# First block of a two-layer trunk kernel: order of its loads, its sum of squares and its projections

## The chip, the cores and the metric

The kernel runs on the 8 cores of one Trainium2 chip. Each core takes one prompt of 2048 tokens and 32 sample tokens, and no core needs another's data. The metric is device time in microseconds of the slowest core, median over runs. A profile is one execution on the slowest core.

## The reference

Two layers, each a mixer and an MLP with residual adds, for 2080 tokens of 1024 channels per core:

```
h = rmsnorm(x, norm1_g)
u, q, k, v, gb, gc, gh = split(h @ w_in)          # 256, 3 x 384, 3 x 384 columns
y_pool = pool_mix(u)                              # window sums over 2, 4, 8, 16 tokens, then 64 x 64 products
y_attn = dilated attention of q, k, v             # three groups of two heads, QK-norm, partial rotary
z = gc * gh;  y_conv = gb * conv_mix(z)           # causal width-3 convolution
x = x + concat(y_pool, y_attn, y_conv) @ w_out
x = x + square(relu(rmsnorm(x, norm2_g) @ w_up)) @ w_down
```

rmsnorm(x, g) is x * rsqrt(mean(x*x) + 1e-6) * g. Each layer also returns the last rows of its pooling, convolution and key/value histories.

## The kernel before, in words

Tokens lie along the free axis, channels on the 128 partitions. The 2080 tokens are cut into 5 blocks of 416 (BL), and a block of x is 8 chunks of 128 channels, one 128x416 tile each. For every block of layer 0 the mixer does this: the chunks of x are loaded; each is scaled by the norm's gain and cast to bf16 into HT (cast1, line 859 on VectorE and GpSimd, 860 on ScalarE); each is squared, and a matmul with a matrix of ones sums the squares over partitions and chunks into one PSUM bank (sumsq, lines 1002 and 1003 for block 0, 1011 and 1012 for the others); ScalarE takes Ln (1054) and Exp (1066) of that sum, which gives 1/rms; and a Square (1103, in rv) gives its square. The projections run on the unnormalised bf16 tile HT: proj (1172) is 8 accumulating matmuls per 128 output columns. Their results are multiplied by 1/rms, or its square, when they leave PSUM. The convolution item (conv_item) first multiplies the "c" projection by the square of 1/rms (1288), then by the "h" projection (1300, 1302), runs the convolution (860, 1313, 1315), multiplies by 1/rms (1318) and by the "b" projection (1322). pool_item does the same for the pooling columns with "p" projections (1228, 1233, 1238, 1251). The token sums (1072) give the same 1/rms per token for the attention's q, k and v, whose projections are line 1357.

All loads of x but two, and all weights, are issued by GpSimd (POOL) on its DMA queue; the weights are cast to bf16 on the way. Block 0 of x is loaded in four quarters of two chunks (load_x, line 939): the first two quarters by SyncE (SP), the last two by GpSimd. Blocks 1 to 4 come in two halves of four chunks. The "c", "h", "p" and "b" weights come as 11 pieces w_a of 128 columns (load_piece, line 964), called c0, h0, c1 and so on. Small loads go by SP: smallc (gains and constants, 922), sconv and spool (histories, 1185 and 1187), qk_g (953). The squares of block 0 are written to Z0, the place of x that later holds V tiles; a memset of those (1803) on GpSimd has to wait until they are read.

The program is emitted by a planner. Items are generators that yield operations with a priority; the planner keeps one queue per engine, models durations and DMA time, and appends whatever is ready and most urgent to that engine's fixed order. An operation given as "any" of several engines goes to the first that is free. Hardware then runs each engine's list in order, with semaphore waits where data or space is shared. So a changed rule or cost moves instructions on all engines far behind the place of the change. Waits of the planner on its own events (ev) order the lists; they make no semaphore wait by themselves.

## Time and profile before

| | |
|---|---|
| median of 3 runs | 1437.58 us (1434.56 to 1439.44) |
| the profiled execution's own time | 1430.84 us |
| its span, slowest core | 1429.3 us (cores 1418.1 to 1429.3) |
| TensorE busy | 1380.4 us, 97% of the span |
| VectorE, ScalarE, GpSimd busy | 821.7, 705.7, 385.1 us |
| share of the chain that ended last on TensorE | 89% |
| mean granted TensorE clock, by core | 0.992 to 0.997 |

The span runs from the first to the last instruction of a core; what is outside it is 1.5 us here. The page has seven parts: busy times, the span in 40 slices, DMA queues, the chain of work that ended last, the costliest groups of instructions and the DMA issues; the trace answers questions on any stretch, tile or line. A load's time to landing counts from the start of its issue. An f32 matmul leaves two records in the trace. A granted clock of 1.00 is 2.4 GHz, 0.50 is 1.2 GHz.

### The profile page before, as it was taken

What the parts mean: (1) busy time and instruction counts of PE and PEld (TensorE: products, weight loads), DVE (VectorE), ACT (ScalarE), POOL (GpSimd) and SP (SyncE); (2) the same over time, 40 slices, a digit from 0 to 9 for tenths busy, and PEclk for the clock granted to TensorE, in tenths of its full rate; (3) what the DMA queues carried; (4) which work ended last, traced back from release to release, by engine and by line L of the source; (5) the groups of instructions that cost most, each with busy time, mean ns of one, the idle gap of its engine ahead of it and who ended that gap; (6) DMA issues with size and microseconds to landing.
All of it is one profiled execution on the core that took longest, in us unless ns stands there. A gap on an engine that the chain in (4) does not pass through costs nothing.

```text
span 1429.3 us, 28093 instructions; the slowest of 8 cores (1418.1 to 1429.3 us)
## 1 busy us (share of the span) xinstructions
PE 1380.4 (97%) x8921; PEld 787.5 (55%) x8921; DVE 821.7 (57%) x1534; ACT 705.7 (49%) x1495; POOL 385.1 (27%) x561
## 2 busy tenths in 40 slices
PE   6999998899999999999999999899999999999998
PEld 2555665455555555555555566555555555555554
DVE  1878876774444444446677788867644444444443
ACT  3657665664244342436646566557444343433522
POOL 4566747340000000002236666653000000000000
PEclk8999999999999999999999999999999999999999
DMA  9851447960652490143245052399037228200122
GB/s 202 204 83 33 89 107 166 230 89 1 120 77 77 92 180 1 19 85 95 73 98 126 26 88 55 95 261 164 3 82 114 77 64 133 76 1 1 49 97 96
DMA packets 81679, 133.33 MB, mean 93 GB/s; under 512 B 14008, under 2 KB 70520, under 8 KB 81152
## 3 DMA queue, kind: packets, MB, share of 16 engines
q0 software_dynamic: 53952, 79.29, 30.4%
q1 hardware_dynamic: 18880, 49.10, 11.6%
q10 hardware_dynamic: 8704, 3.15, 0.9%
q8 instruction: 75, 1.23, 0.4%
q14 instruction: 68, 0.56, 0.1%
HBM read 159.63 MB, written 47.90 MB: 145 GB/s over the span
## 4 chain that ended last, share of the span: by engine, by line
PE 89%; DMA 4%; issue 2%; POOL 2%; DVE 1%; ACT 1%; SPq 0%; DVEq 0%; POOLq 0%; ACTq 0%
PE psum L1767 32%; PE psum L1743 31%; PE psum L1357 9%; PE psum L1172 9%; PE psum L1720 4%; DMA big<-xin 1%; PE psum L1589 1%; DMA big<-xin_r 1%; POOL big L859 1%; DMA big<-xpark 1%; PE psum L1480 1%; DMA kv_p<-big 1%; PE psum L1003 1%; PE psum L1564 0%; PE psum L1614 0%
## 5 line engine op out<-in xcount | busy, mean ns | idle before, releaser
L1743 PE MATMUL psum<-big 128*128 128x416 bf16 x2560 | 457.6, 339 | 2.3 <-DVE big L1755 1.5
L1767 PE MATMUL psum<-big 128*128 128x416 bf16 x2560 | 456.6, 339 | 0.0
L1743 PEld LDWEIGHTS psum<-big 128*128 128x128 bf16 x2560 | 249.2, 98 | 202.7 <-issue 6.2
L1767 PEld LDWEIGHTS psum<-big 128*128 128x128 bf16 x2560 | 249.8, 98 | 199.8 <-issue 1.7
L1758 ACT ACTIVATE big<-big 128x416 f32<-128x416 f32 x291 | 159.6, 549 | 403.8 <-DVE big L1755 402.9
L1755 DVE TENSOR_TENSOR big<-psum,big 128x416 f32<-128x416 f32 x320 | 188.8, 591 | 231.5 <-PE psum L1743 173.5
L1770 DVE TENSOR_TENSOR big<-psum,big 128x416 f32<-128x416 f32 x320 | 189.0, 591 | 226.7 <-PE psum L1767 226.1
L1759 ACT ACTIVATE big<-big 128x416 bf16<-128x416 f32 x320 | 175.0, 549 | 49.0 <-POOL big L1757 6.1
L1172 PE MATMUL psum<-big 128*128 128x416 bf16 x880 | 172.3, 345 | 5.5 <-ACT big L1093 1.4
L1357 PE MATMUL psum<-big 128*128 128x384 bf16 (+1 forms) x816 | 140.5, 326 | 2.3 <-ACT big L1576 2.3
L860 ACT ACTIVATE big<-big 128x416 bf16<-128x416 f32 (+5 forms) x139 | 87.3, 636 | 82.6 <-DVE big L1724 36.1
L1172 PEld LDWEIGHTS psum<-big 128*128 128x128 bf16 x880 | 83.7, 100 | 72.1 <-issue 14.0
L975 POOL DMA_DIRECT2D big<-w_up x32 | 24.6, 777 | 312.7 <-PE psum L1743 301.7
L1357 PEld LDWEIGHTS psum<-big 128*128 128x128 bf16 (+1 forms) x816 | 77.7, 98 | 53.6 <-issue 4.1
L1720 PE MATMUL psum<-big 128*128 128x416 bf16 x480 | 86.9, 339 | 7.5 <-DVE big L1724 7.5
L859 POOL TENSOR_SCALAR big<-big 128x416 bf16<-128x416 f32 (+5 forms) x43 | 60.7, 1413 | 86.3 <-DVE big L1724 30.8
L1720 PEld LDWEIGHTS psum<-big 128*128 128x128 bf16 x480 | 46.2, 98 | 45.6 <-issue 10.6
L1724 DVE TENSOR_TENSOR big<-psum,big 128x416 f32<-128x416 f32 x80 | 46.1, 587 | 30.1 <-PE psum L1720 22.5
L1419 POOL TENSOR_TENSOR big<-big 128x128 f32<-128x128 f32 (+1 forms) x87 | 48.0, 552 | 28.6 <-DVE big L1418 15.5
L1424 ACT ACTIVATE big<-psum 128x512 f32<-128x512 f32 (+1 forms) x54 | 30.7, 569 | 48.3 <-PE psum L1357 44.5
L975 POOL DMA_DIRECT2D big<-w_down x32 | 24.4, 773 | 72.9 <-PE psum L1767 72.9
L1313 DVE SCALAR_TENSOR_TENSOR big<-big 128x416 f32<-128x416 f32 (+1 forms) x60 | 41.2, 693 | 1.4 <-POOL big L859 0.4
(144 smaller groups left out, 1155.2 us busy)
## 6 DMA issues: line engine op xcount, KB each, us to landing
big<-w_up POOLq DMA_DIRECT2D x32, 512.0 KB, 13.5
big<-w_down POOLq DMA_DIRECT2D x32, 512.0 KB, 10.5
kv_s<-c SPq DMA_DIRECT2D x8, 2040.0 KB, 12.4
big<-xin_r POOLq DMA_DIRECT2D x10, 832.0 KB, 8.7
xpark<-big SPq DMA_DIRECT2D x10, 832.0 KB, 4.1
big<-xpark POOLq DMA_DIRECT2D x10, 832.0 KB, 13.9
yout<-big SPq DMA_DIRECT2D x20, 416.0 KB, 2.4
big<-xin POOLq DMA_DIRECT2D x8, 832.0 KB, 13.0
```

The costliest lines, as they stand in the source:

```text
L859: f = lambda e: e.tensor_scalar(out=out, in0=in_, scalar1=g, scalar2=None, op0=ALU.mult)
L860: return anyof(act(n, lambda e: e.activation(out=out, in_=in_, func=AF.Copy, scale=g), r, w, True), dvec(n, f, r, w), pool(n, f, r, w, False))
L975: yield ops(ldc(lambda e: e.dma_start(out=dst, in_=src), 1048576, 2048, w=[(nm, i, h)], slot=(nm, i, h)))
L1172: bi = yield late(1, lambda bi: pe([(BL, lambda e, d=d: e.matmul(bank(bi)[:, 0:BL], lhsT=wa(l, nm, i, d), rhs=HT[:, d, BL * b:BL * b + BL] ...
L1357: pb0 = yield late(J, lambda pb0: pe([(384, lambda e, d=d, j=j, jj=jj: e.matmul(bank(pb0 + jj)[0:R, 0:384].rearrange("p (k n) -> p k n", k ...
L1720: bi = yield late(1, lambda bi: pe([(BL, lambda e, c=c: e.matmul(bank(bi)[:, 0:BL], lhsT=WO[c // 2][:, c % 2, 128 * oc:128 * oc + 128], rh ...
L1743: bi = yield late(1, lambda bi: pe([(BL, lambda e, d=d: e.matmul(bank(bi)[:, 0:BL], lhsT=WU[i][:, d, 128 * fc:128 * fc + 128], rhs=HT[:, d ...
L1755: yield ops(dve(BL, lambda e: e.tensor_tensor(out=rl, in0=bank(bi)[:, 0:BL], in1=VB[v], op=ALU.mult), [("ps", bi), kvb(v)], [kr]))
L1758: yield ops(anyof(act(BL, lambda e: e.activation(out=rl, in_=rl, func=AF.Relu), [kr], [kr]), dvec(BL, f, [kr], [kr]), pool(BL, f, [kr], [k ...
L1759: yield ops(act(BL, lambda e: e.activation(out=AT[a][:, fc, :], in_=rl, func=AF.Square), [kr], [("at", a, fc)]))
L1767: bi = yield late(1, lambda bi: pe([(BL, lambda e, f=f: e.matmul(bank(bi)[:, 0:BL], lhsT=WD[i][:, f, 128 * oc:128 * oc + 128], rhs=AT[a][: ...
L1770: yield ops(dve(BL, lambda e: e.tensor_tensor(out=X[:, s, oc, :], in0=bank(bi)[:, 0:BL], in1=X[:, s, oc, :], op=ALU.add), [("ps", bi), ("x ...
```

## The change

It has five parts. (1) SP's second quarter of x is issued right behind the first: sconv, spool and qk_g are held by the planner until all of block 0's loads are done in its model. (2) The squares of block 0 are added in pairs on VectorE, and four f32 matmuls with ones take the place of eight. (3) Block 0's casts may go to ScalarE and VectorE, no longer to GpSimd. (4) Weight pieces h0 and c1 are issued ahead of block 1 of x. (5) The "h" projection of block 0's convolution items is its own item, which needs neither the norm nor the history. The planner's model of early DMA time is also changed (a factor of 1.35 and a floor at 3.3 us).

```diff
--- before.py
+++ after.py
@@ -457,9 +457,12 @@
         self.busy[eng] += cost
         if len(op) > 4 and eng != "dve":
             t, n, d = op[4]
-            if max(self.dma_free, self.now) < 4.5:
-                t *= 2.0
-            if eng == "pool":
+
+            cold = self.now < 4.5 and t > 1.0
+            if cold:
+                t *= 1.35
+                self.dma_free = max(self.dma_free, 3.3)
+            if eng == "pool" or cold:
                 self.dma_free = max(self.dma_free, self.now) + t
                 self.bulk = d
                 done = self.dma_free + 2.0
@@ -996,13 +999,16 @@
         if l == 0 and which == 0 and b == 0:
 
             bi = yield acq(BANKS)
-            for c in range(8):
-                yield wait(src[c])
-                t, k = Z0[:, 0, c, :], ("x", SV, c)
-                yield ops(act(BL, lambda e: e.activation(out=t, in_=X[:, si, c, :], func=AF.Square), [("x", s, c)], [k]))
-                K.spawn(later(pe([(BL * 4, lambda e, c=c, t=t: e.matmul(bank(bi)[:, 0:BL], lhsT=ONESR[:, :].bitcast(F32), rhs=t, start=(c == 0), stop=(c == 7)),
-                                   ["onesr", k], [("ps", bi)])]), ev("nadd", l, which, b, c)), 1)
-            yield wait(*[ev("nadd", l, which, b, c) for c in range(8)])
+            def pair(c):
+                t, k, t0, k0 = Z0[:, 0, c, :], ("x", SV, c), Z0[:, 0, c - 1, :], ("x", SV, c - 1)
+                yield wait(src[c - 1], src[c])
+                yield ops(*[act(BL, lambda e, t_=t_, c_=c_: e.activation(out=t_, in_=X[:, si, c_, :], func=AF.Square), [("x", s, c_)], [k_]) for t_, k_, c_ in ((t0, k0, c - 1), (t, k, c))])
+                yield ops(dve2(BL, lambda e: e.tensor_tensor(out=t, in0=t, in1=t0, op=ALU.add), [k, k0], [k]))
+                yield ops(pe([(BL * 4, lambda e: e.matmul(bank(bi)[:, 0:BL], lhsT=ONESR[:, :].bitcast(F32), rhs=t, start=(c == 1), stop=(c == 7)), ["onesr", k], [("ps", bi)])]))
+                K.fire(ev("nadd", l, which, b, c))
+            for c in (1, 3, 5, 7):
+                K.spawn(pair(c), 2 if c < 7 else 1)
+            yield wait(*[ev("nadd", l, which, b, c) for c in (1, 3, 5, 7)])
         elif l == 0 and which == 0:
             bi = yield acq(BANKS)
             for c in range(8):
@@ -1034,7 +1040,8 @@
 
         yield wait(src, *before)
         o, i = HT[:, c, BL * b:BL * b + BL], X[:, si, c, :]
-        yield ops(scaled(BL, o, i, NG[:, l, 0, c:c + 1], [("x", s, c), "ng"], [("ht", b, c)]))
+        op = scaled(BL, o, i, NG[:, l, 0, c:c + 1], [("x", s, c), "ng"], [("ht", b, c)])
+        yield ops(anyof(*op[1][:2]) if l == b == 0 else op)
         K.fire(ev("hc", l, b, c))
 
     def cast_watch(l, b):
@@ -1180,7 +1187,7 @@
         return ap.rearrange("p (r n) -> p r n", n=4)
 
     def load_hist(l, s):
-        yield wait(ev("free", l, s))
+        yield wait(*([ev("free", l, s)] if l else [ev("xr", 0, 0, c) for c in range(8)]))
         if s == SC:
             yield ops(ld(lambda e: e.dma_start(out=ZS[:, 0:2], in_=sconv[l]), 12288, 96, w=[("zs", cc) for cc in range(3)], slot="zs"))
         else:
@@ -1279,6 +1286,13 @@
         Zv = Z[cc]
         kz, ks = ("z", cc), ("zs", cc)
         cw = lambda k: CONVW[:, l, cc, k:k + 1]
+        hb = []
+
+        def ahead():
+            hb.append((yield from proj(l, "h", cc, b)))
+        if l == b == 0:
+
+            he = K.spawn(ahead(), 1000)
         bc = yield from proj(l, "c", cc, b)
         yield wait(ev("rv", l, b))
         ci = yield acq(PCA)
@@ -1296,7 +1310,11 @@
         K.fire(ev("cg", l, b, cc))
         if b == 0:
             yield wait(ev("hist", l, SC))
-        bh = yield from proj(l, "h", cc, b)
+        if l == b == 0:
+            yield wait(he)
+        else:
+            hb.append((yield from proj(l, "h", cc, b)))
+        bh = hb[0]
         o2 = [dve(L, lambda e: e.tensor_tensor(out=Zv[:, 2:2 + L], in0=bank(bh)[:, o:BL], in1=gs[:, o:BL], op=ALU.mult), [("ps", bh), kg], [kz])]
         if b == 0:
             o2.append(dve(32, lambda e: e.tensor_tensor(out=ZS[:, 2:10, cc, :], in0=n4(bank(bh)[:, 0:32]), in1=n4(gs[:, 0:32]), op=ALU.mult), [("ps", bh), kg], [ks]))
@@ -1806,7 +1824,7 @@
     def mixer(l):
         base = 1000 * l
         K.spawn(zero_q(l), base + 1)
-        K.spawn(seq([] if l == 0 else [ev("qk", l - 1, blk, g, pr) for blk in range(4) for g in range(3) for pr in range(2)] + [ev("qk", l - 1, None, g, 0) for g in range(3)], load_gqk(l)), base + 1)
+        K.spawn(seq([ev("xr", 0, 0, c) for c in range(8)] if l == 0 else [ev("qk", l - 1, blk, g, pr) for blk in range(4) for g in range(3) for pr in range(2)] + [ev("qk", l - 1, None, g, 0) for g in range(3)], load_gqk(l)), base + 1)
         K.spawn(v_ones(l), base + 1)
         for s in (SC, SP_):
             K.spawn(load_hist(l, s), base + 0.01)
@@ -1910,7 +1928,7 @@
     K.spawn(consts(), 0)
     x_loads = lambda b: [load_x(b, h) for h in range(2 if b else 4)]
     w = lambda *a: [load_piece(0, x[0], int(x[1])) for x in a]
-    K.spawn(loads([], 0, *x_loads(0), *w("c0"), *x_loads(1), *w("h0", "c1", "h1", "c2", "h2"), *w("p0", "p1", "b0"), load_pw(0), *w("b1", "b2"),
+    K.spawn(loads([], 0, *x_loads(0), *w("c0", "h0", "c1"), *x_loads(1), *w("h1", "c2", "h2"), *w("p0", "p1", "b0"), load_pw(0), *w("b1", "b2"),
                   *x_loads(2), *x_loads(3), load_atc(), *[load_wq(0, i) for i in range(3)], *x_loads(4)), 0)
     K.spawn(loads([ev("ht", 0, 4), ev("sq", 0, 4)], 3, *[load_wo(0, i) for i in range(3)]), 3)
     for l in range(DEPTH):
```

The first place is the start of TensorE's list. Lines 1003 and 1007 are the matmul with ones of block 0's squares (before, and in the changed file), 1172 and 1179 a projection, 1072 and 1079 the token sums, 1012 and 1018 the matmul with ones of block 1. Before:

```order
L1003 MATMUL psum<-big,onesr 128x416 x6
L1172 MATMUL psum<-big 128x416 x8
L1003 MATMUL psum<-big,onesr 128x416 x2
L1072 MATMUL psum<-onesr,big 128x1 x3
L1072 MATMUL psum<-onesr,big 32x1
L1012 MATMUL psum<-sqr,onesr 128x416 x2
L1172 MATMUL psum<-big 128x416 x8
L1012 MATMUL psum<-sqr,onesr 128x416
L1172 MATMUL psum<-big 128x416 x8
```

Now:

```order
L1007 MATMUL psum<-big,onesr 128x416 x2
L1179 MATMUL psum<-big 128x416 x8
L1007 MATMUL psum<-big,onesr 128x416 x2
L1179 MATMUL psum<-big 128x416 x16
L1079 MATMUL psum<-onesr,big 128x1 x3
L1079 MATMUL psum<-onesr,big 32x1
L1018 MATMUL psum<-sqr,onesr 128x416 x3
L1179 MATMUL psum<-big 128x416 x16
```

One projection stood between six and two matmuls with ones; now one stands between two and two, and two more projections (16 matmuls) stand ahead of the token sums, which need the norm's Ln. At the same place VectorE's list; 859 and 862 are casts, 1006 the new add of two squares, 1288 and 1302 the first multiply of a "c" projection. Before:

```order
L859 TENSOR_SCALAR big<-big 128x416 x8
L1288 TENSOR_TENSOR big<-psum,big 128x416 x2
L1300 TENSOR_TENSOR big<-psum,big 128x384
L1302 TENSOR_TENSOR big<-psum,big 128x8x4
L1300 TENSOR_TENSOR big<-psum,big 128x384
```

Now:

```order
L862 TENSOR_SCALAR big<-big 128x416 x2
L1006 TENSOR_TENSOR big<-big 128x416
L862 TENSOR_SCALAR big<-big 128x416
L1006 TENSOR_TENSOR big<-big 128x416
L862 TENSOR_SCALAR big<-big 128x416 x2
L1006 TENSOR_TENSOR big<-big 128x416 x2
L1302 TENSOR_TENSOR big<-psum,big 128x416 x2
```

The eight casts were one run; now the first add stands behind the second cast, which needs the second quarter of x, and the adds alternate with the casts. The second place is the start of GpSimd's list: 939 and 942 are loads of x, 964 and 967 weight pieces, 859 and 862 casts, 1803 and 1821 the memset over the squares. Before:

```order
L939 DMA big<-xin 128x832 x2
L964 DMA big<-w_a 128x1024
L859 TENSOR_SCALAR big<-big 128x416
L939 DMA big<-xin 128x1664 x2
L859 TENSOR_SCALAR big<-big 128x416
L964 DMA big<-w_a 128x1024 x3
L859 TENSOR_SCALAR big<-big 128x416
L964 DMA big<-w_a 128x1024
```

Now:

```order
L942 DMA big<-xin 128x832 x2
L967 DMA big<-w_a 128x1024 x3
L942 DMA big<-xin 128x1664 x2
L967 DMA big<-w_a 128x1024
L1821 MEMSET big 128x8x64
L967 DMA big<-w_a 128x1024
L1819 MEMSET big 128x2x64 x2
L967 DMA big<-w_a 128x1024
L1819 MEMSET big 128x2x64
L862 TENSOR_SCALAR big<-big 128x416
```

Five loads that stood between casts are now issued ahead of any cast; the first cast on GpSimd is one of block 1, with the memset ahead of it. The third place is GpSimd's list at the loads of blocks 2 and 3 of x, 1245 being the first add of the pooling item (1238 before), which waits for VectorE's line 1240 (1233 before). Before:

```order
L939 DMA big<-xin 128x1664
L1290 MEMSET big 128x2
L939 DMA big<-xin 128x1664
L1227 MEMSET big 128x15
L939 DMA big<-xin 128x1664
L1227 MEMSET big 128x15
L939 DMA big<-xin 128x1664
L859 TENSOR_SCALAR big<-big 128x416
L925 DMA big<-atc 128x864
```

Now:

```order
L942 DMA big<-xin 128x1664 x2
L1234 MEMSET big 128x15
L942 DMA big<-xin 128x1664
L1234 MEMSET big 128x15
L1245 TENSOR_TENSOR big<-big 128x398
L942 DMA big<-xin 128x1664
L862 TENSOR_SCALAR big<-big 128x416
L928 DMA big<-atc 128x864
L948 DMA big<-w_q 128x3072
```

The last half of block 3 was issued straight behind a memset; it now stands behind the pooling add, and the loads of the constants (925, 928) and the first w_q (948) behind it.

## Rows read from the trace of the kernel before

**Rows 1.** The page, part 1: engine, busy us (share of the span), instructions
```profile
PE 1380.4 (97%) x8921; PEld 787.5 (55%) x8921; DVE 821.7 (57%) x1534; ACT 705.7 (49%) x1495; POOL 385.1 (27%) x561
```

**Rows 2.** Windows view: stretch, its length, busy of five engines, PEclk, DMA share, GB/s
```profile
14.00:17.00 3.00, 1.94 (x3) 1.17 (x4) 1.26 (x4) 3.00 (x7) 0.27 (x1) 0.53 0.99 323
17.00:20.70 3.70, 3.70 (x6) 1.50 (x5) 1.68 (x4) 1.18 (x3) 3.70 (x6) 0.50 1.03 190
...
24.00:27.90 3.90, 1.74 (x10) 1.27 (x11) 0.00 (x0) 3.71 (x11) 1.98 (x7) 0.99 1.06 164
27.90:30.40 2.50, 2.49 (x9) 1.13 (x9) 0.59 (x1) 1.19 (x3) 0.00 (x0) 0.50 1.11 159
...
82.40:300.00 217.60, 204.59 (x1728) 123.75 (x1727) 168.79 (x334) 140.09 (x340) 128.97 (x199) 0.99 0.57 119
```

**Rows 3.** Timeline of the first 7 us, loads of x (start, duration, engine)
```profile
1.66 1.30 POOL L939 DMA_DIRECT2D big<-xin  x2 [0.25 <-issue]
...
2.93 0.43 SPq L939 DMA_DIRECT2D big<-xin  x1
```

**Rows 4.** DMA view, loads issued at 1.6 to 8.6 us: KB, us to landing
```profile
big<-xin POOLq DMA_DIRECT2D x1, 416.0 KB, 6.8
big<-xin POOLq DMA_DIRECT2D x1, 416.0 KB, 8.4
big<-xin SPq DMA_DIRECT2D x1, 416.0 KB, 10.8
big<-w_a POOLq DMA_DIRECT2D x1, 256.0 KB, 11.0
...
big<-xin POOLq DMA_DIRECT2D x1, 832.0 KB, 8.0
```

**Rows 5.** Timeline of 13 to 29 us; brackets: idle time before, and its releaser
```profile
13.84 0.64 ACT L860 ACTIVATE big<-big 128x416 bf16<-128x416 f32 x1 [5.97 <-DMA big<-xin]
15.06 5.89 PE L1003 MATMUL psum<-big,onesr 128*128 128x416 f32 x8 [4.38 <-ACT big L1002]
22.27 1.56 PE L1003 MATMUL psum<-big,onesr 128*128 128x416 f32 x4
23.98 0.61 ACT L1054 ACTIVATE big<-psum,big 128x416 f32<-128x416 f32 x1 [5.80 <-PE psum L1003]
24.73 0.95 PE L1072 MATMUL psum<-onesr,big 128*128 128x1 f32 x8 [0.91 <-ACT big L1054]
26.34 0.16 ACT L1092 ACTIVATE big<-psum 128x3 f32<-128x3 f32 x1
27.68 0.53 ACT L1011 ACTIVATE sqr<-big 128x416 fp32r<-128x416 f32 x1
27.91 2.93 PE L1172 MATMUL psum<-big 128*128 128x416 bf16 x8 [1.44 <-ACT big L1093]
28.75 0.59 DVE L1288 TENSOR_TENSOR big<-psum,big 128x416 f32<-128x416 f32 x1 [8.65 <-ACT big L1103]
```

**Rows 6.** The chain that ended last, 31 to 83 us: start, us, what
```profile
31.19 1.50 PE psum L1172 x8
...
59.45 10.13 DMA big<-xin
...
82.59 2.62 PE psum L1357 x16
```

**Rows 7.** Timeline of VectorE at 38 and 42 us
```profile
38.03 0.58 DVE L1318 TENSOR_TENSOR big<-big 128x416 f32<-128x416 f32 x1
...
42.61 0.54 DVE L1233 TENSOR_TENSOR big<-psum,big 128x384 f32<-128x384 f32 x1
```

**Rows 8.** DMA view, loads issued at 23.2, 24.8 and 25.4, 56.4 us
```profile
big<-w_a POOLq DMA_DIRECT2D x1, 256.0 KB, 12.7
big<-xin POOLq DMA_DIRECT2D x2, 832.0 KB, 19.6
big<-w_q POOLq DMA_DIRECT2D x1, 768.0 KB, 8.8
```

## Prediction

> **What bounds the kernel now.** First the page's busy times: TensorE is busy 1380.4 us of a span of 1429.3 [rows 1], so 48.9 us of idle time, and the matmuls that ran at the lower clock, are all that a new order can win. Next the windows, which say where these lie: from 82.4 to 300 us TensorE idles 217.60 - 204.59 = 13.0 us; from 14 to 30 us it is half idle or at 0.50 to 0.53 of its clock (1.2 GHz) most of the time [rows 2]. A change that touches only the first block of layer 0 directly must earn its time there and keep it through the rest of that layer's mixer.
>
> Then the timeline of the start. A load's landing is its issue plus its time. GpSimd's two quarters of x, issued together from 1.66 to 2.96 (the second near 2.3), took 6.8 and 8.4 us and were there at 8.5 and 10.7; SP's second quarter, issued at 2.93 behind two small loads, took 10.8 and landed at 13.7 [rows 3, 4]. ScalarE's cast at 13.84 had idled 5.97 us for it, and TensorE idled 4.38 us for the squares behind it. TensorE then did eight records (four f32 matmuls) in 5.89 us, the first projection, and from 22.27 the last four records; the norm's Ln started at 23.98 and VectorE's first multiply only at 28.75, for ScalarE had put other work between Ln and the Square on which it waits [rows 5]. The chain gives the state at 32.7 us (31.19 + 1.50) [rows 6]: TensorE has then done block 0's sums of squares and token sums, three projections and three squares of block 1. I call this the mark; the changed list of TensorE, read above, holds the same set up to its third matmul of block 1.
>
> **The change step by step.** All times are estimates from these rows.
>
> *SP's second quarter.* It is issued at about 1.95, and shares the DMA engines with GpSimd's quarters alone. Nearest row: GpSimd's second quarter, as large and second in its queue as well, landed at 10.7; I take that. Bounds: 8.5 (GpSimd's first quarter) and 13.7 (no change) [rows 4]. The trace shows what the small loads do to a queue only by this one load. sconv, spool and qk_g now share with c0: it landed at 2.94 + 11.0 = 13.9 beside the same loads, and I leave it there.
>
> *Pairs instead of eight matmuls.* Four adds on VectorE at 0.58 us (line 1318, same form [rows 7]), which was 1.26 us busy in the 3 us from 14 [rows 2]: no cost, but the first add stands behind the cast that waits for the second quarter. So: cast 10.7 to 11.1, add to 11.7, second add at 12.7, the last at about 15.4. Two matmuls with ones are four records of 0.74 us at the lower clock (5.89/8), from 11.8 to 14.7. The first projection needs c0 (13.9) and casts that are done by 13.6, and costs 2.93 us at the lower clock (line 1172 at 27.91 [rows 5]), to 17.6. Before, the records ahead of that projection ran at 0.50 of the clock [rows 2] and the four behind it took 0.39 us each, the higher clock's price [rows 5]; with the same order of work I take the same prices, so 1.56 us for the last two matmuls, to 19.2. Ln starts 0.15 us later, as it did before (22.27 + 1.56 to 23.98), at 19.3.
>
> The casts taken from GpSimd go to ScalarE and VectorE, which wait for x there. No cost.
>
> *Ln to the first multiply.* ScalarE's list now has Ln, Exp and Square in a row: 0.61 + 2 x 0.53 and 0.3 of waits, so VectorE's multiply starts near 21.3 instead of 28.75, 7.4 us earlier.
>
> *Projections ahead of the norm.* h0 and c1 stand behind c0 on the DMA queue. Four quarters and c0 (4 x 416 KB and 512 KB, cast to 256 on the way) had landed at 13.9, some 200 KB per us from 3 us on; so 2.6 us each: 16.5 and 19.1. TensorE needs them at 19.2 and 20.7. Sixteen matmuls, 2 x 1.50 [rows 6]: to 22.2; token sums, 0.95 [rows 5]: to 23.1. Here a wait is new: the third square of block 1 stands on ScalarE behind the reads of the token sums, and from the first of these (26.34) to that square's end (27.68 + 0.53) took 1.9 us before [rows 5]; one more square of 0.53 and waits follow, so its matmul ends at 26.2. Block 1's first half, landing at 8.55 + 8.0 = 16.6 before, has two pieces ahead of it now: 21.8 at most, in time. The mark is reached at 26.2, **6.5 us earlier**. With the bounds of the second quarter this is 7.3 (c0 then holds the projection) or 3.5; if the clock stayed at 0.50 throughout, 5.86 instead of 3.0 for two projections and 2.95 instead of 1.56 make it 2.2.
>
> On clock and gaps the Trainium skill, "TensorE: Matmul & The Clock Gate", section "HAM oscillation — how this bites in real kernels", says that waits between groups of matmuls throttle the array again. By that rule the new wait near 24 us speaks for the low end, 2.2; the rows agree in kind (0.50 at 27.9, after 1.74 us busy out of 3.9 [rows 2]), but the one fall in these rows came after longer idle time, so I stay with the higher clock and count the low end with the first rival below.
>
> *GpSimd's queue.* Issuing h0, c1 and block 1 at once, earlier than before, costs nothing: the DMA engines are 0.99 to 1.11 busy from 14 to 30 us [rows 2] either way. The last pieces land as before, b2 at 23.2 + 12.7 = 35.9 [rows 8]; shifted by 6.5 us TensorE wants it near 39. The last half of block 3 now stands behind the pooling add, thus behind VectorE's line 1233, at 42.61 before [rows 7]. With 7.4 us off and some 3 us of block 1's casts put in between, that is 38.3, issue at 39.5. It was issued at 25.4 and landed near 45.0 (the two halves' median was 19.6 us [rows 8]) for want of DMA bandwidth, not for its issue. After 39.5 and another 8.0, the time of block 1's first half, it lands at 47.5: 2.5 us later, in a chain with room: the third w_q landed at 56.4 + 8.8 = 65.2 and the last block of x at 59.45 + 10.13 = 69.6, both held by late issues from GpSimd, while the attention's first projection came at 82.59 [rows 6, 8]. At zero, then.
>
> *The rest.* Behind the mark all lists are shuffled as far as layer 0's MLP. I see nothing that TensorE does more or less of; I take 0.5 us off for new waits. **Sum: 6.5 - 0.5 = 6.0 us**, against the profiled execution's 1430.84: 1424.8. That execution lies 6.7 us below the median of the runs shown; against the median, 1437.58 - 6.0 = **1431.6 us**. A measurement of this kernel tells a change from none at about 0.3%, 4.3 us.
>
> **Rivals.**
>
> *Given back.* DMA work is the same and was never idle early; if x and w_q, not TensorE's start, time what comes up to 82.6, the 6.5 us turn into waits before it. For it: DMA busy above 0.99 [rows 2], the late loads [rows 6, 8]. Against it: 13 us lie between the last block's landing and the attention's start. Also here: half of the gain lost to a shuffled attention stage. Also here: a clock that stays low, 2.2 us less waits. Left: about 1.5 us, 1436. The Trainium skill, "DMA: Bandwidth & Descriptors", section "Issuing engines are not separate DMA queues", says that loads of all issuing engines interleave on the same 16 DMA engines, so that another queue or an earlier issue saves only the issue; by that rule the second quarter gains only what the small loads lose. Only SP's one load (10.8 beside 8.4) bears on it here.
>
> *The small loads are not held.* The lists make no semaphore wait for them, so they run behind the second quarter at once, beside c0. Were c0 3 us later for it, the projection and the mark would be too: 6.5 - 3 = 3.5, 1434.1, the low end of the forecast's own range, where I count it with a chance of 0.08.
>
> *More.* The attention stage idles 13.0 us; a start 7 us earlier for VectorE, with 168.79 of 217.6 us busy there [rows 2], may take a third of it as well: 6.0 + 4 = 10, 1427.6.
>
> *Slower: the pooling add holds the loads.* GpSimd's queue runs dry if the add comes after 36 us (block 3's first half lands near 24.8 + 19.6 = 44.4, less 8.0). If VectorE reaches line 1233 at 45.6, that is 42.61 and the 3 us of casts with no gain before, block 3's half is issued near 47 and lands at 55; three w_q of 4.8 us (1.5 MB at the 323 GB/s of [rows 2]) end at 70 instead of 65.2, and block 4's first half lands at 73 instead of 69.6. With casts and squares behind it TensorE loses some 5 us: 1442.6. Against it: VectorE's start hangs on the second quarter and c0 alone. It decides when the add comes later than about 43.
>
> **How the numbers follow.** Forecast (gain of 3.5 to 9 us, 1428.6 to 1434.1): 0.50 with the small loads' case, of which 0.44 is beyond 4.3 us. Given back: 0.30, all within 0.3%. More: 0.10. Slower: 0.10, all beyond it. Faster 0.44 + 0.10 = 0.54, same 0.06 + 0.30 = 0.36, slower 0.10. The range, 1424.5 to 1441.5, takes in the forecast, nearly all of "given back", most of "more" and the milder "slower" cases.
>
> **What would show it.** Right: SP's second quarter lands by 11; four new adds and eight f32 records; Ln near 19.3; VectorE's first multiply near 21.3; the mark near 26; the attention's first projection near 76; and from 82 on no more idle time than 13 us. Wrong: Ln after 22 with the second quarter still late, or the first projection of attention within 2 us of 82.6 (given back), or a dry DMA queue between 44 and 50 us (slower).

## The result, and the profile after

The changed kernel takes **1426.61 us** (median of three runs, 1426.24 to 1426.70) beside 1438.38 for the kernel before (four runs, 1434.56 to 1439.44): a ratio of 0.9922, 95% interval 0.9899 to 0.9946, so about 11.2 us less by the ratio (8 to 14.5). Executions in which a die was disturbed are left out of all medians here, and for e2 and e9 below, whose profiled execution was one of them, the profile's figures are means over the four cores of the other die. On the three chips of the experiments (e1 to e4, e5 to e8, e9 to e12) the kernel before had medians of 1433.5 to 1433.9, and the changed one, measured again beside e6 to e8, 1425.61: 8.2 us less, ratio 0.9942 (0.9927 to 0.9956). Forecast were 6.0 us less. The profiled execution took 1426.61 us, its span is 1425.1.

Busy times hardly moved, by 3.3 us at most, as against [rows 1]. Page of the changed kernel, part 1:

```profile
PE 1378.4 (97%) x8913; PEld 787.2 (55%) x8913; DVE 825.0 (58%) x1531; ACT 708.4 (50%) x1501; POOL 381.8 (27%) x562
```

Windows of the changed kernel, columns as in [rows 2]; the last stretch begins at its first attention projection and is as long as that of before:

```profile
14.00:17.00 3.00, 3.00 (x8) 1.06 (x7) 1.19 (x2) 0.86 (x2) 2.03 (x6) 1.00 1.05 221
17.00:20.70 3.70, 3.70 (x16) 2.02 (x15) 0.00 (x0) 1.09 (x2) 0.65 (x1) 1.00 1.00 334
24.00:27.90 3.90, 2.88 (x8) 1.51 (x9) 2.54 (x8) 3.35 (x10) 3.90 (x10) 0.58 1.08 172
...
72.20:289.80 217.60, 202.32 (x1706) 122.64 (x1705) 166.15 (x324) 140.65 (x345) 123.59 (x198) 0.99 0.60 118
```

From 14 to 20.7 us TensorE now works without a gap, where it had idle time or worked at half clock. The 1.00 of the first of these rows is not borne out by its matmuls: the first projection takes 2.92 us for eight (below), the price that the kernel before paid at 0.50 (2.93 at 27.91 [rows 5]), and sixteen behind it take 2.98. At 24 us there is a new hole, and the clock falls behind it (0.58). In the long stretch it idles 15.3 us, where it was 13.0.

Timeline of the start, the changed kernel's core 0; it answers to [rows 3, 5]. Line 1061 is Ln, 1302 the first multiply, 1018 the second block's matmul with ones:

```profile
1.51 0.90 SPq L942 DMA_DIRECT2D big<-xin  x2
...
11.05 0.64 ACT L863 ACTIVATE big<-big 128x416 bf16<-128x416 f32 x1 [1.91 <-DMA big<-xin]
...
12.14 3.11 PE L1007 MATMUL psum<-big,onesr 128*128 128x416 f32 x4 [12.14 <-DVE big L1006]
...
15.05 2.92 PE L1179 MATMUL psum<-big 128*128 128x416 bf16 x8
...
17.80 1.56 PE L1007 MATMUL psum<-big,onesr 128*128 128x416 f32 x4
...
19.20 2.98 PE L1179 MATMUL psum<-big 128*128 128x416 bf16 x16
...
19.51 0.61 ACT L1061 ACTIVATE big<-psum,big 128x416 f32<-128x416 f32 x1 [4.66 <-PE psum L1007]
...
21.51 0.59 DVE L1302 TENSOR_TENSOR big<-psum,big 128x416 f32<-128x416 f32 x1 [5.95 <-ACT big L1110]
...
25.02 1.12 PE L1018 MATMUL psum<-sqr,onesr 128*128 128x416 f32 x2 [1.74 <-ACT sqr L1017]
...
25.94 4.01 PE L1179 MATMUL psum<-big 128*128 128x416 bf16 x16
```

The second quarter is cast at 11.05 instead of 13.84, Ln comes at 19.51 instead of 23.98, the multiply at 21.51 instead of 28.75, and the third matmul of the second block's squares (the mark) ends at 25.02 + 1.12 = 26.14 instead of 32.7.

GpSimd's list around the last half of block 3, changed kernel:

```profile
37.23 1.05 POOL L1245 TENSOR_TENSOR big<-big 128x398 f32<-128x398 f32 x1 [9.27 <-DVE big L1240]
38.23 0.58 POOL L942 DMA_DIRECT2D big<-xin  x1
...
46.31 1.58 POOL L862 TENSOR_SCALAR big<-big 128x416 bf16<-128x416 f32 x1 [1.62 <-DMA big<-xin]
...
56.92 0.60 POOL L942 DMA_DIRECT2D big<-xin  x1
...
57.97 0.58 POOL L942 DMA_DIRECT2D big<-xin  x1
```

The pooling add holds the load, as foreseen, until 38.23; what it brings is there at 46.3. The last block of x is issued at 56.92 and 57.97, where [rows 6] has 59.45.

The third view to read is that of the cores, for the metric is the slowest of eight. Kernel before, then the changed one:

```profile
core 0: 1419.7 us, clock 0.997
core 1: 1427.9 us, clock 0.992
core 2: 1427.2 us, clock 0.993
core 3: 1418.2 us, clock 0.996
...
core 6: 1429.3 us, clock 0.993
core 7: 1418.1 us, clock 0.993
```

```profile
core 0: 1425.1 us, clock 0.995
core 1: 1418.1 us, clock 0.997
core 2: 1423.8 us, clock 0.995
core 3: 1416.8 us, clock 0.995
...
core 6: 1420.0 us, clock 0.996
core 7: 1424.6 us, clock 0.996
```

Of each pair (0 and 1, 2 and 3, and so on) one core ends late, now the one, now the other. Over 26 executions of the kernel before (those beside the first four experiments) the quicker core of a pair has a mean of 1420.4 us, the slower of 1430.0, and the slowest of the eight 1432.2. Over the five of the changed kernel beside the fifth these are 1417.4, 1422.8 and 1424.0: the quicker ones gained 3.0 us, the slower ones 7.2, the slowest of the eight 8.2.

### The profile page after: what moved, and what is told of

Its sections match the earlier page's. It is cut to its first block, busy times and chain, and to the rows that moved or that the text cites. A ratio compares the mean times of both kernels' runs of the same rounds, so it can differ in the third digit from the quotient of the medians.

```text
span 1425.1 us, 28092 instructions; the slowest of 8 cores (1415.6 to 1425.1 us)
## 1 busy us (share of the span) xinstructions
PE 1378.4 (97%) x8913; PEld 787.2 (55%) x8913; DVE 825.0 (58%) x1531; ACT 708.4 (50%) x1501; POOL 381.8 (27%) x562
## 4 chain that ended last, share of the span: by engine, by line
PE 87%; DMA 5%; POOL 2%; issue 2%; DVE 2%; ACT 2%; DVEq 0%; ACTq 0%; SPq 0%; POOLq 0%
PE psum L1785 32%; PE psum L1761 31%; PE psum L1179 8%; PE psum L1375 8%; PE psum L1738 4%; DMA big<-xin 2%; PE psum L1607 1%; DMA big<-xin_r 1%; POOL big L862 1%; DMA big<-xpark 1%; DMA big<-vspill 1%; PE psum L1498 1%; ACT big L1442 0%; PE psum L1582 0%; PE psum L1079 0%
## 5 line engine op out<-in xcount | busy, mean ns | idle before, releaser
L1375 PEld LDWEIGHTS psum<-big 128*128 128x128 bf16 (+1 forms) x816 | 77.9, 98 | 55.5 <-issue 7.0
L862 POOL TENSOR_SCALAR big<-big 128x416 bf16<-128x416 f32 (+5 forms) x41 | 56.8, 1388 | 75.1 <-DVE big L1742 38.0
L1742 DVE TENSOR_TENSOR big<-psum,big 128x416 f32<-128x416 f32 x80 | 46.4, 588 | 28.5 <-PE psum L1738 18.4
L1437 POOL TENSOR_TENSOR big<-big 128x128 f32<-128x128 f32 (+1 forms) x83 | 45.4, 546 | 20.1 <-DVE big L1436 10.3
## 6 DMA issues: line engine op xcount, KB each, us to landing
big<-xpark POOLq DMA_DIRECT2D x10, 832.0 KB, 14.5
```

The lines of the kernel that those rows point to most:

```text
L862: f = lambda e: e.tensor_scalar(out=out, in0=in_, scalar1=g, scalar2=None, op0=ALU.mult)
L1375: pb0 = yield late(J, lambda pb0: pe([(384, lambda e, d=d, j=j, jj=jj: e.matmul(bank(pb0 + jj)[0:R, 0:384].rearrange("p (k n) -> p k n", k ...
```

## The experiments

Three theories stood at the start. A: the gain is the earlier front (the work of the first block up to the mark), the same on all cores. B: what decides is the landing of the last block of x, on the slower core of each pair. C: it is the new order of the attention stage.

Most edits move instructions in the finished lists and leave all others where they are; waits follow the data. The table gives means over the cores of the profiled execution: the mark here is the time when five projections of the first block and five matmuls of the second block's squares are done (it suits all orders), then the first and the last attention projection; the last column is the median time.

| kernel | mark | first | last | median us |
|---|---|---|---|---|
| before (profiled as above) | 35.3 | 80.3 | 227.5 | 1433.5 to 1433.9 |
| changed (profiled as above) | 29.6 | 70.8 | 223.2 | 1426.6 |
| e1 before, last block of x earlier | 35.8 | 78.5 | 224.8 | 1430.6 |
| e2 before, SP's new order (cores 0 to 3) | 31.7 | 78.7 | 226.0 | 1431.8 |
| e3 changed, SP's old order | 31.5 | 70.9 | 223.2 | 1426.5 |
| e4 changed, held | 33.3 | 73.1 | 225.7 | 1429.2 |
| e5 changed, again | 28.5 | 69.6 | 222.1 | 1425.6 |
| e6 changed, nothing ahead of the norm | 33.1 | 73.9 | 226.2 | 1428.9 |
| e7 changed, no pairs | 30.1 | 70.3 | 223.3 | 1427.3 |
| e8 changed, last block of x earlier | 28.4 | 68.4 | 219.8 | 1424.4 |
| e9 changed, four parts undone (cores 4 to 7) | 38.1 | 79.2 | 231.9 | 1436.9 |
| e10 changed, lists dealt anew | 29.2 | 69.7 | 215.3 | 1432.8 |
| e11 e8 and squares first | 27.8 | 68.8 | 220.1 | 1426.1 |
| e12 e8 and x read again earlier | 28.8 | 68.0 | 219.5 | 1422.4 |

**e1**, GpSimd's list of the kernel before:

```diff
+L939 DMA big<-xin 128x1664 x2
 L945 DMA big<-w_q 128x3072
...
-L939 DMA big<-xin 128x1664 x2
```

> The kernel before, with one thing moved: the two loads of the fifth block of x stand on GpSimd's queue ahead of the third load of w_q and of the pooling work behind it, nothing else. Theory A (the front): the gain comes from the first block's norm being over earlier; nothing before 55 us is touched here, so the time stays that of the kernel before, 1438 us within 1.5. Theory B (the landing): on the cores that end last, the attention's first projection (82 to 83.4 us on four cores, 78 on the other four) hangs on the landing of the fifth block (69.6 on core 6, 65.8 on core 0); issued some 3 us earlier it lands by 66.5 on every core, all cores come to the first projection by 79.5, and the slowest core's time falls by 3 to 5 us, to 1433 to 1435. A third view (the third part of w_q is now the late one): the same or slower, with the tensor engine waiting for that load at 85 to 95 us.

The cores did come together at the first attention projection: 76.8 to 79.5 us instead of 77.9 to 83.4. Casts of the last block, core 0 and core 6 of e1:

```profile
64.33 1.83 POOL L859 TENSOR_SCALAR big<-big 128x416 bf16<-128x416 f32 x1 [4.17 <-DMA big<-xin]
```

```profile
64.30 1.33 POOL L859 TENSOR_SCALAR big<-big 128x416 bf16<-128x416 f32 x1 [3.66 <-DMA big<-xin]
```

Before, core 0 had its first half at 65.98 and core 6 at 69.75. So theory B is right up to 80 us. At the end the median is 3.3 us less (1430.6 beside 1433.9), the lower end of what B said: eight of the nine executions lie at 1429.3 to 1431.5. The ninth took 1447.3; with it the ratio, 0.9991 (0.9966 to 1.0015), can't be told from nothing. The two profiled executions do not show the gain: they took 1430.87 and 1430.84 us, the latter near the lowest of the 26 (1430.4), and the last output projection starts at 276.5 to 284.5 in e1, at 277.2 to 285.2 before. Where the lead gets to behind the attention stays open.

**e2 and e3**, SP's list, the same exchange in the one kernel and undone in the other:

```diff
 L939 DMA big<-xin 128x832
+L939 DMA big<-xin 128x832
 L1185 DMA big<-sconv 128x24
 L1187 DMA big<-spool 128x120
-L939 DMA big<-xin 128x832
```

> The kernel before, with one thing moved: on SP's queue the second quarter of x stands directly behind the first, ahead of the loads of sconv and spool. Theory A: the second quarter lands near 11 instead of 13.7, the squares and the eight matmuls with ones that wait for it run up to 2.7 us earlier, Ln starts at 21.3 to 22.5 instead of 23.98, and the third matmul of the second block's squares near 30 instead of 32.7; all that follows keeps this, 1438 becomes 1435 to 1436. Theory B: GpSimd's queue and the landing of the fifth block move by under 1 us, and the time by under 1 us. If the two old queue neighbours cost nothing, the second quarter lands at 13.7 as before and nothing moves.

> The changed kernel, with SP's queue as before the change: the loads of sconv and spool stand between the first and the second quarter of x, nothing else. Theory A: the second quarter lands near 13.7 instead of 11.0, the last pair's work on it is 2.7 us later, Ln moves from 19.5 to 21.5 or later, the third matmul of the second block's squares from 26.1 to 28 or 29, and the time from 1426.6 to 1428.5 to 1429.5. Theory B: the time stays within 1 us of 1426.6, since the fifth block of x still lands near 65.5. A third view (the first block's order of quarters is such that the second one isn't the last): Ln stays at 19.5 and nothing moves.

e2: Ln at 20.9 on core 1, where that core had 23.6; the mark 3.6 us earlier, the time 2 us less (ratio 0.9988, 0.9976 to 1.0001, which just reaches no change), at the low end of theory A's 2 to 3. But the landing of the last block's first half moved as well, from 67.1 to 65.2 in the mean of these four cores, where B expected under 1 us: the front moves that landing, and A and B are not independent. e3 misses theory A's number: the second quarter came late, Ln at 21.82 on core 5 (19.32 in the changed kernel), the mark 3 us later than in e5, but the first attention projection and the time stay within 1.3 us. Three microseconds at the mark are worth 0.8 there, as theory B has it. Timeline of e3, core 5:

```profile
14.16 0.64 ACT L863 ACTIVATE big<-big 128x416 bf16<-128x416 f32 x1 [5.36 <-DMA big<-xin]
...
21.82 0.61 ACT L1061 ACTIVATE big<-psum,big 128x416 f32<-128x416 f32 x1 [3.85 <-PE psum L1007]
```

**e4**, ScalarE's list:

```diff
+L1005 ACTIVATE big<-big 128x416 x11
 L1005 ACTIVATE big<-big 128x416 x2
```

> The changed kernel, with ScalarE held for some 6 us ahead of the first block's first square (it computes that square eleven times more, each behind the one before), all lists otherwise the same. Theory A: Ln goes from 19.5 to near 25.5, the third matmul of the second block's squares from 26.1 to near 32.5, the attention's first projection from 72 to 78, and the time from 1426.6 to 1432.5 to 1433: each microsecond of the front is one of the end. Theory B: the hold costs at the end what it does to the landing of the fifth block of x; if GpSimd still issues it before 58 us and it lands by 66.5, the time rises by under 2 us. Theory C (the order of the attention stage is what gained): the time rises by under 3 us whatever the front does, since idle time in the attention stage takes the rest up.

The hold was partly covered, since the second quarter lands at 10.7 anyway: Ln moved by 2.6 us on core 1 (19.11 to 21.73) and 3.9 on core 5. Against e5 the mark is 4.9 us later, the first attention projection 3.5, the time 3.6. About three quarters pass.

**e5**, no edit.

> The changed kernel itself, with the same lists on every engine, beside the kernel before on one chip: what the difference is here, core by core. Theory B (the slower core of each pair): the quicker core of each pair (0 and 1, 2 and 3, ...) gains 2 to 3 us against the kernel before, the slower one 5 to 6, and the slowest of the eight 7 to 8: near 1426.6 where the kernel before has 1434. Theory A alone (the front, the same for all cores): all cores gain the same 6.5 us.

As theory B has it (numbers above): not all cores gain alike. That fits B; it does not by itself show that the last block of x is the cause.

**e6**, TensorE's list:

```diff
-L1179 MATMUL psum<-big 128x416 x16
 L1079 MATMUL psum<-onesr,big 128x1 x3
 L1079 MATMUL psum<-onesr,big 32x1
-L1018 MATMUL psum<-sqr,onesr 128x416 x3
-L1179 MATMUL psum<-big 128x416 x16
+L1018 MATMUL psum<-sqr,onesr 128x416 x2
+L1179 MATMUL psum<-big 128x416 x8
+L1018 MATMUL psum<-sqr,onesr 128x416
+L1179 MATMUL psum<-big 128x416 x24
```

> The changed kernel, with two projections (h0 and c1 of the first block) put back behind the token sums and the second block's first squares on the tensor engine, where the kernel before has its second and third projection; nothing else moves. The tensor engine then stands idle for some 3 us between the last matmul with ones and the token sums, and three projections and three squares' matmuls are done near 29 instead of 26.1. Theory A': two thirds of a delay there come out at the end (as the 2.7 to 4.0 us of the hold gave 2.1 to 2.6): 1428 to 1429. Theory B: the first attention projection stays within 1 us of 70.6, since the fifth block of x still lands near 65.5, and the time within 1 us of 1426.6.

1428.9: 3.3 us more, theory A'. TensorE now waits four times, for the norm's Ln, for a read of the token sums and twice for squares (core 4):

```profile
18.76 0.95 PE L1079 MATMUL psum<-onesr,big 128*128 128x1 f32 x8 [0.91 <-ACT big L1061]
...
20.64 0.42 PE L1018 MATMUL psum<-sqr,onesr 128*128 128x416 f32 x1 [0.93 <-ACT big L1099]
...
22.41 0.69 PE L1018 MATMUL psum<-sqr,onesr 128*128 128x416 f32 x1 [1.35 <-ACT sqr L1017]
22.90 2.92 PE L1179 MATMUL psum<-big 128*128 128x416 bf16 x8
...
31.42 0.87 PE L1018 MATMUL psum<-sqr,onesr 128*128 128x416 f32 x2 [1.18 <-ACT sqr L1017]
```

The projection behind the third of these runs at half clock (2.92 for eight; 0.53 granted from 22.9 to 25.8). Projections ahead of the norm are the dearest of the three parts that were undone alone.

**e7**, TensorE's and VectorE's lists (all four adds go, and each of the two pairs of matmuls with ones becomes four):

```diff
-L1006 TENSOR_TENSOR big<-big 128x416
...
-L1007 MATMUL psum<-big,onesr 128x416 x2
+L1007 MATMUL psum<-big,onesr 128x416 x4
```

> The changed kernel without the pairs: VectorE's four adds are gone and the tensor engine has the eight f32 matmuls with ones again, four of them behind the first projection; the sum is taken in another order, all else stands. The two matmuls more behind the first projection take 1.5 us by the 0.78 us of one there, less the 0.6 us of the add that nobody waits for: Ln near 20.4 instead of 19.5, and the third matmul of the second block's squares near 27. Theory A': 0.6 us at the end, 1427.2. Theory B: nothing, within 0.5 us of 1426.6. If the matmuls at the low clock (1.45 us each at 12 to 15 us) do not fit ahead of the first projection, Ln comes at 22 or later and the time rises by 1.5 us.

1427.3, 1.7 us more than e5, nearly three times what A' said. Ln lay between 17.8 and 21.2 us on the eight cores (18.0 to 19.5 in the changed kernel). It goes with the price of the first projection: 1.57 us for eight matmuls on cores 0, 1, 3, 4 and 5, and 2.66 to 2.80, nearly that of the lower clock, on cores 2, 6 and 7. The windows grant 1.00 in these stretches on core 0 and on core 2 alike, so what the price hangs on is not shown.

**e8**, GpSimd's list of the changed kernel:

```diff
+L942 DMA big<-xin 128x1664 x2
 L948 DMA big<-w_q 128x3072
...
-L942 DMA big<-xin 128x1664
...
-L942 DMA big<-xin 128x1664
```

> The changed kernel, with the two loads of the fifth block of x ahead of the third load of w_q on GpSimd's queue, as in the first experiment. Theory B: in the changed kernel the fifth block's landing (65.5 on every core) is still what the tensor engine waits for at 66 (1.2 to 2.2 us on five cores); it lands by 63, that wait goes, the attention's first projection starts near 69 instead of 70.6, and the time is 1 to 2 us less, 1424.6 to 1425.6. Theory A': no difference. A third view (contention at the end): the cores gain at 70 us and give it back where x is read again behind the attention, at 250 to 265 us, since both cores of a pair come there together: the time stays within 1 us.

1424.4 (1422.5 to 1424.8; e5 has 1425.0 to 1425.9): 1.2 us less, and the first attention projection at 68.4 instead of 69.6. Theory B holds here to the end, but the load's first half landed 4.7 us earlier (59.4 instead of 64.1 in the mean), so that landing is not all that holds the attention's start.

**e9**, e3, e6 and e7 together, and on GpSimd's queue the second block's loads of x ahead of those of h0 and c1, as before the change:

```diff
 L967 DMA big<-w_a 128x1024
+L942 DMA big<-xin 128x1664 x2
 L967 DMA big<-w_a 128x1024 x2
-L942 DMA big<-xin 128x1664 x2
```

> The changed kernel with four parts of the change undone at once, and every other instruction in its place: the small loads of sconv and spool between the quarters of x, the second block's two loads of x ahead of those of h0's and c1's weights, eight matmuls with ones without adds, and h0 and c1 behind the token sums. What stays of the change is the rest of the lists, above all GpSimd's: no casts of the first block of x ahead of its loads, and the new order from 36 us on. Alone, three of the parts cost 0.8, 3.2 and 1.7 us against 1425.7. Theory A'' (the four parts are the whole gain): the time of the kernel before, 1433 to 1434. Theory D (they add up, and the lists hold the rest): 1431.4 or a little more for the fourth part, 1431 to 1432.5, some 2 us under the kernel before. Theory E (they overlap, since the landing of the fifth block of x is a floor): under 1430.

None of the theories: 1436.9, ratio to the kernel before 1.0032 (1.0015 to 1.0049). The four parts are worth 11.2 us together where three of them alone sum to 5.8; the mark moves by 9.6. So the gain hangs on these four parts. The loss seems to grow with the delay: 3.0 at the mark cost 0.8 (e3), 4.9 cost 3.6 (e4), 9.6 cost 11.2; but the fourth part was not run alone, so how much of the 11.2 is its own is not shown. And e9 is no copy of the kernel before: the changed lists with the old front reach the mark 2.8 us later than that does.

**e10**, the planner's margin:

```diff
-SLACK = 0.8
+SLACK = 0.9
```

> The changed kernel, with one constant of the planner moved (the margin that it allows a wait of the tensor engine, 0.9 instead of 0.8 us): the first ten rows of the tensor engine's list and all that the change wrote stand as they are, the lists behind are dealt anew. It says what new lists by themselves do to the time. Theory D and theory A (new lists by themselves are worth little): within 1.5 us of 1425.7. Theory C (the order of the lists is what gained): 3 us or more off it, on either side, with the first attention projection away from 70 or the stretch from the first to the last of them away from 152.

Theory C's number: 1432.8, 7.2 us more, with the same front. Yet the attention got quicker; its projections span 145.6 us instead of 152.5. The time is lost in one wait behind it, of 7.6 to 11.7 us on the eight cores (the longest for the same in e5: 3.0). Waits of TensorE from 200 to 290 us, e10, core 0 (us in total, times, longest):

```profile
PE psum L1738 <- DVE big L1742: 11.7, 1, 11.7
```

Line 1742 adds the output projection to x, which is read again for it (xin_r). GpSimd issues that late, for it waits itself:

```profile
239.20 5.19 POOL L1172 DMA_DIRECT2D big<-xin_r  x7 [4.83 <-DVE big L1660]
```

and the chain goes through the landing; TensorE resumes at 250.82, at first at the lower clock (0.50 granted from 251 to 255; 11.40 us for 50 matmuls, where e8 has 5.43 for 30):

```profile
239.20 10.65 DMA big<-xin_r
```

**e11**, e8 and ScalarE's list; 1099 and 1100 read the token sums:

```diff
+L1017 ACTIVATE sqr<-big 128x416 x2
+L863 ACTIVATE big<-big 128x416
 L1017 ACTIVATE sqr<-big 128x416
 L1099 ACTIVATE big<-psum 128x3
 L1100 ACTIVATE big<-psum,big 128x3
-L863 ACTIVATE big<-big 128x416
 L1099 ACTIVATE big<-psum 32x1
 L1100 ACTIVATE big<-psum,big 32x1
-L1017 ACTIVATE sqr<-big 128x416 x2
```

> The changed kernel with two moves: the fifth block's loads ahead of the third load of w_q (1424.4 by itself), and on ScalarE the second block's second and third square ahead of the four reads of the token sums. The new wait of the tensor engine for the third square (1.74 us) falls to 0.5 us or less, the third square's matmul ends near 25 instead of 26, and by the full pass of the front (3.2 us at the end for some 3 at the mark) the time falls by another 1 us: 1423 to 1424. If the reads of the token sums, which free a bank of PSUM, are wanted at once, a projection behind them waits instead and the time stays at 1424.4 or rises.

A miss: the third square's matmul ends 1.5 us earlier (23.3 in the mean of the cores, 24.7 in e5), but the mark only 0.6, and the time is 1426.1 (1422.9 to 1426.5), no less than e8's. What is won there does not reach the end.

**e12**, e8 and GpSimd's list behind the attention (1172 is here the load that reads x again):

```diff
 L1172 DMA big<-xin_r 128x4x416
+L1172 DMA big<-xin_r 128x4x416 x3
 L978 DMA big<-w_down 128x4x512
 L862 TENSOR_SCALAR big<-big 128x416
 L978 DMA big<-w_down 128x4x512
 L1031 TENSOR_TENSOR sqr<-sqr 128x416
-L1172 DMA big<-xin_r 128x4x416 x3
```

> The changed kernel with the fifth block's loads ahead of the third load of w_q (1424.4 by itself), and with three of the loads that read x again behind the attention moved ahead on GpSimd's queue: they stand behind the fourth of them, in front of a load of w_down, two casts' work and another load of w_down, instead of behind all these. In the run of 1424.4 they are issued at 248.99, and the tensor engine waits for what they bring and the load before them brings, three times, 4.2 us in all, between 245 and 262 (core 1). Theory F (the reading again of x is the floor behind the attention, as in the run with new lists, where it made one wait of 11.7 us): they are issued by 242 and land by 256, one or two of the three waits go, the last output projection starts some 2 to 3 us earlier, and the time falls by 1.5 to 3 us, to 1421.5 to 1423. Against it: the queue is full there (DMA share 0.86 to 0.96), so the loads may land no earlier, or the fourth one later; then 1424.4 within 1 us. If the waits of the moved loads hold GpSimd itself (its next cast is wanted at 243), the casts behind come later and the time rises by 1 us.

As theory F has it: 1422.45 (1421.0 to 1423.3), ratio to the kernel before 0.9927 (0.9913 to 0.9941), 3.2 us less than the changed kernel in e5. Waits for the reading again of x, core 1 of e8 and of e12, from 216 to 290 us (core 1 is the best case; in the mean of the cores these waits fall from 3.6 us to 2.2):

```profile
PE psum L1738 <- DVE big L1742: 4.2, 3, 2.6
```

```profile
PE psum L1738 <- DVE big L1742: 1.4, 2, 0.9
```

It is the best of all versions here.

## Why the prediction was right, and where it was not

**The front, step by step, was right.** SP's second quarter: said 10.7, used at 11.05. Adds: said free; they took 0.58 to 0.59 us each, and TensorE went from the first matmuls to the first projection (15.05, said 14.7) without a gap. First projection to 17.8 (17.6), last matmuls with ones to 19.2 (19.2), Ln 19.51 (19.3), multiply 21.51 (21.3), mark 26.14 (26.2). The new wait for the third square is there, 1.74 us. (These are core 0's times, the latest of the eight to reach the mark; the mean over the cores is 25.5.) GpSimd's late half was issued at 38.23 (39.5) and had landed by 46.3 (47.5), so "slower: the pooling add holds the loads" did not come about; c0 was in time beside the small loads, so that rival fell too.

**The size was right in part by luck: three terms were off, of both signs.** The 1426.6 lies below the forecast's own bounds (1428.6 to 1434.1) and inside the wider range; the 8.2 us of the second comparison lie inside the forecast's gain of 3.5 to 9. Two of the signs named for "right" failed: the first attention projection came at 72.2 on core 0, not near 76, and the stretch behind it idles 15.3 us, more than 13. By the profiled executions' means over the cores, the change gains 5.7 us at the mark of the table, 9.5 at the first attention projection, 4.3 at the last one.

*"A chain with room ... At zero, then"* misread the stretch behind the landing. The chain of [rows 6] goes through this load, and the 13 us up to the attention's first projection are no slack but GpSimd's casts and VectorE's work behind them. Chain of the kernel before, core 6 behind the landing, then the load on core 0, and the load on core 6 of the changed kernel:

```profile
69.75 1.90 POOL big L859
...
76.47 1.34 POOL big L859
...
80.84 1.57 PE psum L1172 x8
```

```profile
58.08 7.73 DMA big<-xin
```

```profile
55.18 10.23 DMA big<-xin
```

The load stands in the chain up to the attention on all eight cores before and on seven of eight after (not on core 0). What was read from core 6 alone is the time: the last block of x landed at 69.6 there, at 65.8 on core 0. In the mean of the cores its first half landed at 67.2 before and at 65.5 after, because it was issued earlier (58.7 and 55.5). e1 shows what an earlier landing is worth in the old lists: 1.8 us at the first projection, 4 on the late cores, 3.3 in the median. Of the 9.5, then, 5.7 may be the front and 1.8 the last block, if both pass in full and do not overlap; this sum is an estimate, and what makes the other 2 was not tried.

*"The rest", 0.5 us for new waits*, was too small, and the rival "given back" true in part: the new lists take 152.4 us from the first attention projection to the last, where it was 147.2. That gives 5.2 us back, nearly all of it idle time of TensorE (10.3 us in this stage in the mean of the cores, 5.5 before). "More" (the stage itself gets shorter) was wrong. e10 shows how loose that stage is: other lists do it in 145.6 and lose more behind it.

*The median was taken to follow the profiled execution.* Between the profiled executions lie 4.2 us (1430.84 and 1426.61); between the medians 8.2 to 11.2. The kernel before scatters by 7.6 us (1430.4 to 1438.0 in 26 executions; by 3.6 in the six beside e5), the changed one by 0.9 in five, and the handicap of the slower core of each pair fell from 9.6 us to 5.4. A working for one core could not see that. Why the first comparison has 3 us more than the later ones is open; it has four executions of the kernel before.

**How much the front is worth** was not measured apart from the new lists. Kernels with nearly the same lists give an estimate: e5 at a mark of 28.5 takes 1425.6, e4 at 33.3 takes 1429.2, e9 at 38.1 takes 1436.9. Between the last two, at the 35.3 of the kernel before, a straight line gives 1432.4, so some 6.8 us for the front, near the 6.0 forecast; but this leans on e9 and its fourth part. By e4 and e6 alone, where seven tenths of a delay at the mark came out, it would be 5.

The traces show by which way the front comes through, and there theories A and B are one. In the changed kernel and e3 to e7 the first half of the last block lands at 64.1 to 68.3 us in the mean of the cores, in general the later the later the mark, and the first attention projection follows it by 5.2 to 5.6 us in each of them. (In the kernel before it follows by 13.1, and in e8, where the load is issued ahead of its turn, by 9.0.) So what stands is: the gain hangs on the front; the front moves the landing of the last block of x, and with it the attention's start; x read again is what TensorE waits for behind the attention in e10 and e12. That some seven tenths or more of a delay reach the end holds for e4, e6, e7 and e9, not for e3 (0.8 of 3.0). How the 8.2 us divide between the front, the last block and the other lists is not shown.

On the clock: behind the new wait, sixteen matmuls took 4.01 us on core 0 (above) and 2.97 on core 4, after the same wait of 1.74 us:

```profile
23.47 0.87 PE L1018 MATMUL psum<-sqr,onesr 128*128 128x416 f32 x2 [1.74 <-ACT sqr L1017]
24.25 2.97 PE L1179 MATMUL psum<-big 128*128 128x416 bf16 x16
```

The Trainium skill, "TensorE: Matmul & The Clock Gate", section "HAM oscillation — how this bites in real kernels", says that waits between groups of matmuls throttle the array again; core 0 agrees (0.50 granted from 25 to 28 us), core 4 does not (1.00 throughout); of the eight cores five fell (0, 1, 3, 5 and 7). The low end that the forecast drew from it (2.2 us) did not come.

## What to carry to other kernels

A change at the start is worth its time at the next landing that everyone waits for, not at the next matmul: list those landings (here the last block of x at 65, x read again at 250) and ask of each whether the work or the load comes last, on the slowest core and on the quickest. A load that stands in the chain has no room, however long the stretch behind it is. Where a planner deals the lists anew, as much can be won or lost behind the change as by it (e10, 7.2 us); compare with lists in which only the one thing moves. When the metric is the slowest of several cores, read the spans of all of them before a term is put at zero.

## What the runs showed of the hardware that was not expected

With two small loads (12 and 60 KB) between the two quarters of x on SP's queue, the second quarter was issued about 1.0 us later (2.93 in e3, near 1.95 in the changed kernel) and cast 3.4 us later (14.16 and 10.75 on core 5). The Trainium skill, "DMA: Bandwidth & Descriptors", section "Issuing engines are not separate DMA queues", says that another issuing engine saves only the time of the issue; it speaks of several engines, and the forecast's step from there to an earlier issue did not hold: here the place within one engine's queue was worth three times the issue. With that place changed the order towards GpSimd's two quarters, issued from 1.66 to 2.95; which of the two makes it was not tried.

The two cores of a pair (0 and 1, 2 and 3, 4 and 5, 6 and 7) end 9.6 us apart in the mean of 26 executions of the kernel before; the same cores paired in other ways end 5.3 to 6.2 us apart. Which of the two is the late one changes from one execution to the next. What the two share was not tried by itself.
